# First mixer of a two-block transformer: attention heads, gate chunks and branch product interleaved in rounds

## The chip, the cores and the metric

One core of one Trainium2 chip runs the whole program in one launch. The metric is the device time of that execution in microseconds (us); three executions of the kernel before took 1167.99 to 1169.90 us, with a median of 1169.39 us.

## The reference, cut to what matters

The input is one sequence of 256 tokens by 1024 channels, all in float32. Two blocks follow one another. The change touches only the mixer of the first block:

```python
z, xbc, dt_raw, q, k, v, gate_logits = split(u @ w_in)
y_ssd = ssd_branch(z, xbc, dt_raw, ...)              # ends in (256 x 2048) @ ssd_w_branch (2048 x 1024)
s = (q_m @ k_m.T) * scale - slope[h] * distance      # 8 heads, two maps m, causal
p = softmax(s)
out = (p[0] - lam * p[1]) @ v                        # per head, 256 x 128
y_att = rmsnorm(out, subln_g) * (1 - lam_init) @ da_w_branch
gates = sigmoid(gate_logits + gate_b)                # 2 x 1024 columns
merged = gates[0] * y_ssd + gates[1] * y_att
h = h + rmsnorm(merged @ w_out, mix_post_g)
```

## The kernel before

Tokens lie in two tiles of 128 (t = 0, 1). Every large matrix product is made with operands split in a high and a low part and three matmuls per tile (`parts`, L1479 to L1481), each 128x128 by 128x512. The weights come in units of 128x2048 elements (1 MB) through a ring of five slots. For each unit the queue of SyncE issues a load, once the unit five before it is used (`w_used`). ScalarE then copies the high part (`split_hi`, L437) and VectorE subtracts it to get the low part (`split_lo`, L913). Both engines take the units in order, at places written out by hand in their programs. TensorE waits for `w_lo`. One unit is 24 matmuls, 12 for each tile. In this document a block is one such group of 12.

Nothing plans the order at run time: each engine has one program and works through it in order, and semaphores tie them together.

In the stretch that the change touches, before its first line, the ring has 71 units split on both engines, and units 66 and 67 (gate chunk 0) are already multiplied and kept. Then come, in the kernel before:

- the eight differential heads, one per step of a loop (`for h in range(9)`, L658 on ScalarE, L1168 on VectorE, L1720 on TensorE). VectorE adds the distance table and takes maxima (L1178 to L1182, "max" below), ScalarE takes the exponentials (L670, "exp"), VectorE normalizes and subtracts the two maps (L1190 to L1198, "diff"), TensorE turns the result (three transposes, L1726), ScalarE copies it (L661, "keep"), TensorE multiplies by V (L1739 to L1741, "values"), VectorE copies the result out (`o_keep`, L1165) and ScalarE squares it (L679). The map `SMAP`, the buffer `ATT`, the copy `PT` and the bank `PS[6]` exist once each.
- in the same steps, the SSD branch product: eight units of `ssd_w_branch`, one per head. The operand is turned by TensorE into `PS[7]` (four transposes, L1619), split by `kt_hi` (L530) and `kt_lo` (L1002), and multiplied by `rows` with both tiles (24 matmuls in one go).
- after the heads, the gate chunks 1 to 3, two units each, in one go each. VectorE adds the bias (L1248), ScalarE takes the sigmoid (L694), and VectorE multiplies the SSD branch by its gate into `V` (`first_merge`, L1212).
- then the attention branch's four units (`by_pairs(8, U_DAW, ...)`), the second merge, and `w_out`'s four units.

On ScalarE a head's step is: keep, `kt_hi`, `split_hi`, exp, squares. On VectorE it is: `kt_lo`, max, `split_lo`, `o_keep`, diff. So ScalarE splits before it waits for the maxima of the head.

A later part of the kernel, the second block's mixer, has its own sixteen heads in a loop of 18 rounds (`for q in range(18)`), where three heads are under way at once and a block of 12 matmuls stands between the scores of one head and the values of another. There the VectorE splits stand mostly one round behind those of ScalarE.

Of the kernel before, what the change touches and what calls it, by code (L numbers as in the profile page):

```python
# [113 lines left out]
CHUNK[U_GATE0] = len(CHUNK)  # L114
CHUNK.update({U_GATE + 2 * i: len(CHUNK) + i for i in range(3)})
# [69 lines left out]
def program(nc, w, out):  # L185
    with ExitStack() as ctx:
# [238 lines left out]
        def _(act):  # L425
# [229 lines left out]
            kt_hi(0, 0)  # L655


            for h in range(9):  # L658
                if h:
                    act.wait_ge(p_turned, h)  # L660
                    nc.scalar.activation(PT, PS[6][:, 0:384], ACT.Copy).then_inc(p_kept, 1)  # L661
                if h < 8:
                    if h:
                        kt_hi(h, U_SSDW + h - 1)
                        split_hi()
                    act.wait_ge(s_ready, h + 1)
                    for m in range(2):
                        for i, ks in enumerate((slice(0, P), slice(P, 3 * P))):
                            n = 2 * i + m
                            ins = nc.scalar.activation(SMAP[:, m, ks], SMAP[:, m, ks], ACT.Exp, scale=0.125,  # L670
                                                       bias=SM[:, 4 + n:5 + n], accum_out=SM[:, 8 + n:9 + n])
                            if i == 0:
                                own.inc(ins)
                        ins.then_inc(p_exp, 1)
                if h:
                    act.wait_ge(o_kept, h)
                    for i in range(NT):
                        own.wait()
                        own.inc(nc.scalar.activation(SQJ[:, i * P:(i + 1) * P], XN[:, i, (h - 1) * P:h * P], ACT.Square,  # L679
                                                     accum_out=SS[:, i * 8 + h - 1:i * 8 + h]))  # L680
            split_hi()
            rsqrt(RS[:], SS[:], 1, o_rs, 1.0 / P)


            nc.scalar.preload_act_table(ACT.Sigmoid)
            for n in range(4):
                if n == 3:
                    kt_hi(8, U_DAW - 1, SUBLN)
                if n:
# [210 lines left out]
        def _(dve):  # L900
# [257 lines left out]
            kt_lo(0)  # L1158
# [9 lines left out]
            for h in range(9):  # L1168
                if h < 8:
                    if h:  # L1170
                        kt_lo(h)

                    dve.wait_ge(scores, h + 1)
                    if h:
                        own.wait()
                    f = -8.0 * slopes[h]
                    for m in range(2):
                        own.inc(stt(SMAP[:, m, :], tab("dist"), f, PS[4 + m][:, 0:384], ALU.mult, ALU.add))  # L1178
                    own.wait()
                    own.inc(nc.vector.tensor_reduce(SM[:, 0:2], SMAP[:, :, 0:P], AX.X, ALU.max))  # L1180
                    own.link(nc.vector.tensor_reduce(SM[:, 2:4], SMAP[:, :, P:3 * P], AX.X, ALU.max))
                    ts(SM[:, 4:8], SM[:, 0:4], -0.125, None, ALU.mult).then_inc(s_ready, 1)  # L1182
                    if h:
                        split_lo()
                if h:
                    o_keep(h - 1)
                if h < 8:

                    dve.wait_ge(p_exp, 2 * (h + 1))
                    own.link(nc.vector.reciprocal(SM[:, 12:16], SM[:, 8:12]))  # L1190
                    own.link(ts(SM[:, 16:20], SM[:, 12:16], SM[:, 39:40], None, ALU.mult))

                    if h:
                        dve.wait_ge(p_turned, h)
                    own.inc(ts(ATT[:, 0:P], SMAP[:, 0, 0:P], SM[:, 12:13], None, ALU.mult))
                    own.link(ts(ATT[:, P:3 * P], SMAP[:, 0, P:3 * P], SM[:, 14:15], None, ALU.mult))
                    own.inc(stt(ATT[:, 0:P], SMAP[:, 1, 0:P], SM[:, 17:18], ATT[:, 0:P], ALU.mult, ALU.add))
                    stt(ATT[:, P:3 * P], SMAP[:, 1, P:3 * P], SM[:, 19:20], ATT[:, P:3 * P], ALU.mult,  # L1198
                        ALU.add).then_inc(attn_ok, 1)
                    dve.wait_ge(attn_ok, h + 1)  # L1200
# [12 lines left out]

            def second_merge(m, gates, unit):

                def product(b):
                    g = slice(D + (b % 2) * 512, D + (b % 2) * 512 + 512)
                    if m:
                        own.inc(stt(MB[:, b, :], gates[:, b // 2, g], 1.0, PS[b][:], ALU.add, ALU.mult))
                    else:  # L1220
                        own.inc(tt(MB[:, b, :], PS[b][:], gates[:, b // 2, g], ALU.mult))
# [9 lines left out]
                kt_lo(20 if m else 12, 0.5 if m else None)  # L1231
# [7 lines left out]
            for n in range(4):  # L1239
                if n == 3:  # L1240
                    kt_lo(8, SUBLN)
                if n == 0:
                    dve.wait_ge(gate0_kept, 2)
                cols = slice(n * 512, (n + 1) * 512)
                for t in range(NT):
                    if n:
                        chunk_tile(gate_unit(n), gate_unit(n) + 1, t)
                    tt(BUF1[:, t, cols], PS[gate_bank(n, t)][:] if n else BUF1[:, t, cols], GAIN[:, cols],  # L1248
                       ALU.add).then_inc(g_logit, 1)
                if n:  # L1250
                    split_lo()
                    split_lo()
                if n == 2:

                    dve.wait_ge(gates_ok, 2)
                    for b in range(4):
                        first_merge(BUF1, b, acc_read)
# [4 lines left out]
            products(12, U_WOUT, 4, turned=True)  # L1262
# [766 lines left out]
```

## Time and profile before

| | us |
|---|---|
| median of three executions | 1169.39 |
| the profiled execution, its own time | 1170.61 |
| its span, first to last instruction | 1168.8 |
| PE busy in the span | 1123.3 |
| VectorE (DVE) busy | 694.4 |
| ScalarE (ACT) busy | 586.1 |
| stretch that the change touches, last gate 0 matmul to attention branch's first matmul | about 439.5 to 546.2 |

PE is the matmul part of TensorE and PEld its weight load. A group's row gives the start, the duration and in brackets how long the engine sat idle before it and which engine's work ended that. Matmuls overlap one another in this profile: each lasts 0.39 us in the rows and the next begins 0.23 us after it, so that the work of a stretch on PE is read from the starts, and a wait shows as a start that comes later than 0.23 us. The profile's lines are those of the kernel before.

### The profile page before, as it was taken

Reading aid. Unit: us, or ns where it says so; the run is one execution under the profiler, and the core shown is the slowest. Engines: PE = TensorE matmul, PEld = TensorE weight load, DVE = VectorE, ACT = ScalarE, POOL = GpSimd, SP = SyncE. Lnnn points to the kernel's source line nnn. Section 1 sums busy time; section 2 is a strip of 40 time slices with the busy share of each in tenths; the row PEclk is TensorE's granted clock in tenths of the full one; section 3 lists DMA queues with packets and bytes.
Section 4 is the critical chain, followed back from the end, with each engine's and each line's share of the span. In section 5 each row is a group of like instructions: output and inputs, shape, how many; then the busy total and the mean of one; then the engine's idle time right before and its main releaser. Section 6 shows DMA issues by size and latency. Waiting matters only on the chain. (4 is left out here: it accounts for less than half of the span.)

```text
span 1168.8 us, 13926 instructions
## 1 busy us (share of the span) xinstructions
PE 1123.3 (96%) x5748; PEld 942.0 (81%) x5748; DVE 694.4 (59%) x793; ACT 586.1 (50%) x828; POOL 21.4 (2%) x35
## 2 busy tenths in 40 slices
PE   5999999999999999999999999999899999999997
PEld 4888887899989986777778888877778877888886
DVE  4644554676767777776666445446665656555443
ACT  4543434554567765664455434345566535343333
POOL 0000000000001110000000000000000000000000
PEclk9999999899999999999999999999999999999999
DMA  9656653655566544445456565554633345566550
GB/s 306 213 180 189 195 193 115 218 179 180 176 188 199 185 154 167 143 123 184 146 185 210 183 195 195 183 152 140 203 109 126 131 139 182 181 191 197 187 180 36
DMA packets 132206, 202.74 MB, mean 173 GB/s; under 512 B 5760, under 2 KB 98816, under 8 KB 131888
## 3 DMA queue, kind: packets, MB, share of 16 engines
q1 hardware_dynamic: 129328, 190.68, 50.6%
q0 software_dynamic: 2816, 11.18, 2.8%
q8 instruction: 46, 0.75, 0.3%
q14 instruction: 16, 0.13, 0.0%
HBM read 200.76 MB, written 1.08 MB: 173 GB/s over the span
## 5 line engine op out<-in xcount | busy, mean ns | idle before, releaser
L913 DVE TENSOR_TENSOR WL<-RAW,WH 128x2048 fp32r<-128x2048 f32 (+1 forms) x181 | 406.2, 2265 | 111.1 <-ACT WH L437 111.1
L437 ACT ACTIVATE WH<-RAW 128x2048 fp32r<-128x2048 f32 (+1 forms) x181 | 338.5, 1888 | 12.6 <-DMA RAW<-in_w_out 3.7
L1479 PE MATMUL PS<-WH,XTH 128*128 128x512 f32 (+1 forms) x676 | 267.3, 395 | 0.0
L1481 PE MATMUL PS<-WH,XTL 128*128 128x512 f32 (+1 forms) x676 | 263.4, 390 | 0.0
L1480 PE MATMUL PS<-WL,XTH 128*128 128x512 f32 (+1 forms) x676 | 262.8, 389 | 0.0
L1479 PE MATMUL ACC<-WH,KTH 128*128 128x512 f32 (+1 forms) x476 | 188.7, 396 | 5.7 <-DVE WL L913 3.5
L1481 PE MATMUL ACC<-WH,KTL 128*128 128x512 f32 (+1 forms) x476 | 185.8, 390 | 0.0
L1480 PE MATMUL ACC<-WL,KTH 128*128 128x512 f32 (+1 forms) x476 | 185.4, 390 | 0.0
L1481 PEld LDWEIGHTS PS<-WH,XTL 128*128 128x128 f32 x676 | 126.8, 188 | 26.5
L1479 PEld LDWEIGHTS PS<-WH,XTH 128*128 128x128 f32 x676 | 127.0, 188 | 24.9 <-issue 0.5
L1480 PEld LDWEIGHTS PS<-WL,XTH 128*128 128x128 f32 x676 | 127.1, 188 | 24.6
L1479 PEld LDWEIGHTS ACC<-WH,KTH 128*128 128x128 f32 x476 | 89.8, 189 | 26.2 <-DVE WL L913 6.8
L1481 PEld LDWEIGHTS ACC<-WH,KTL 128*128 128x128 f32 x476 | 89.7, 188 | 18.7
L1480 PEld LDWEIGHTS ACC<-WL,KTH 128*128 128x128 f32 x476 | 89.8, 189 | 17.4
L477 ACT ACTIVATE KTH<-PS 128x512 fp32r<-128x512 f32 x33 | 19.7, 597 | 164.2 <-PE PS L1539 164.0
L935 DVE TENSOR_TENSOR KTL<-PS,KTH 128x512 fp32r<-128x512 f32 x33 | 22.8, 690 | 122.0 <-ACT KTH L477 122.0
L487 ACT ACTIVATE SCR<-PS 128x256 f32<-128x256 f32 x66 | 25.3, 384 | 121.3 <-PE PS L1481 121.2
L944 DVE TENSOR_TENSOR SCR<-PS,SCR 128x256 f32<-128x256 f32 x66 | 27.6, 421 | 54.5 <-ACT SCR L487 54.4
L1479 PE MATMUL ACC<-XTH,WH 128*128 128x256 f32 x192 | 55.9, 291 | 0.0
L1480 PE MATMUL ACC<-XTL,WH 128*128 128x256 f32 x192 | 55.4, 288 | 0.0
L1481 PE MATMUL ACC<-XTH,WL 128*128 128x256 f32 x192 | 55.3, 288 | 0.0
L1479 PE MATMUL ACC<-WH,XTH 128*128 128x512 f32 (+1 forms) x120 | 47.5, 396 | 1.9 <-ACT SCR L720 1.9
(264 smaller groups left out, 1283.0 us busy)
## 6 DMA issues: line engine op xcount, KB each, us to landing
RAW<-in_w_in SPq DMA_DIRECT2D x50, 1024.0 KB, 5.2
RAW<-in_ffn_w_gate SPq DMA_DIRECT2D x44, 512.0 KB, 4.0
RAW<-in_ffn_w_up SPq DMA_DIRECT2D x44, 512.0 KB, 5.0
RAW<-in_ffn_w_down SPq DMA_DIRECT2D x22, 1024.0 KB, 4.9
RAW<-in_w_gate SPq DMA_DIRECT2D x22, 512.0 KB, 4.0
RAW<-in_w_up SPq DMA_DIRECT2D x22, 512.0 KB, 5.0
RAW<-in_w_down SPq DMA_DIRECT2D x11, 1024.0 KB, 4.9
RAW<-in_ssd_w_branch SPq DMA_DIRECT2D x8, 1024.0 KB, 5.0
```

Of the source, the lines that this page charges most:

```text
L437: nc.scalar.activation(WH[:, s, 0:n], RAW[:, s, 0:n], ACT.Copy).then_inc(w_hi, 1)
L477: nc.scalar.activation(KTH[:, half_of(j)], PS[6][:], ACT.Copy).then_inc(hT_hi, 1)
L487: nc.scalar.activation(SG[:, t, :], PS[4 + t][:, 0:256], ACT.Silu).then_inc(gate_ok, 1)
L913: tt(WL[:, s, 0:n], RAW[:, s, 0:n], WH[:, s, 0:n].bitcast(F32), ALU.subtract).then_inc(w_lo, 1)
L935: tt(KTL[:, half_of(j)], PS[6][:], KTH[:, half_of(j)].bitcast(F32), ALU.subtract).then_inc(hT_lo, 1)
L944: tt(HS[:, t, :], PS[4 + t][:, 256:512], SG[:, t, :], ALU.mult).then_inc(h_ready, 1)
L1479: mm(ps, stat_hi, mov_hi, start=first, stop=False)
L1480: mm(ps, stat_hi, mov_lo, start=False, stop=False)
L1481: return mm(ps, stat_lo, mov_hi, start=False, stop=last)
```

## The change

The eight heads go into ten rounds, q = 0 to 9, written out by hand. In round q the scores of head q are made, its maxima and exponentials taken; the diff of head q-1 and its transposes; the values, `o_keep` and squares of head q-2. Between these steps stand the blocks of 12 matmuls of gate chunks 1 and 2 (rounds 0 to 2) and of the SSD branch product (rounds 3 to 8). That product now goes by tile in eight steps (two blocks each, over pairs of units, as `by_pairs` does), with operand steps `ssd_turn`, `ssd_kt_hi`, `kt_lo`. Gate chunk 3 follows the heads. The weight units are loaded in the new order: gates 0 to 2, SSD branch, gate 3. The sigmoid becomes (1 + tanh(x/2))/2: the additions of 1 are made in the merges, which were multiplications, and the factor 0.5 is taken in the splits of the operand of `w_out`. The first merge writes over the gates instead of into `V`. The scaling of the attention result by its norm is four instructions instead of one.

The diff, cut: the bodies of the steps on the heads are the old ones under names (`head_max1`, `head_exp1`, `head_diff1`, `head_keep1`, `head_square1`, `head_scores1`, `head_values1`) and are left out, as are most of the removed lines, which stand in the kernel before. The order is ScalarE, VectorE, TensorE.

```diff
-U_SSDW = U_GATE0 + 2
-U_GATE = U_SSDW + 8
-U_DAW = U_GATE + 6
+U_GATE = [U_GATE0, U_GATE0 + 2, U_GATE0 + 4]
+U_SSDW = U_GATE[2] + 2
+U_GATE += [U_SSDW + 8]
+U_DAW = U_GATE[3] + 2
 U_WOUT = U_DAW + 4
...
-return ((4, 0), (4, 5), (6, 7), (4, 5))[n][t]
+return ((4, 0), (1, 7), (2, 3), (4, 5))[n][t]
...
+def ssd_kt_hi(s):
+    if s >= 2 and s % 2 == 0:
+        act.wait_ge(tile_half, HALF[U_SSDW + s - 2])
+    kt_hi(s, U_SSDW + s - 1 if s % 2 else 0)
+def gate_tanh(n, count):
+    act.wait_ge(g_logit, count)
+    a = BUF1[:, :, n * 512:(n + 1) * 512]
+    nc.scalar.activation(a, a, ACT.Tanh, scale=0.5).then_inc(gates_ok, 1)
...
+nc.scalar.preload_act_table_set("exp_and_others")
+for q in range(10):
+    if q < 8:
+        head_exp1(q)
+    if q == 0:
         split_hi()
         split_hi()
+    elif q in (1, 6, 7, 8):
+        split_hi()
+    elif q == 2:
+        split_hi()
+        gate_tanh(1, 2)
+        ssd_kt_hi(0)
+    elif q == 3:
+        split_hi()
+        ssd_kt_hi(1)
+        gate_tanh(2, 4)
+    elif q == 4:
+        ssd_kt_hi(2)
+        split_hi()
+        ssd_kt_hi(3)
+    elif q == 5:
+        split_hi()
+        gate_tanh(0, 6)
+        ssd_kt_hi(4)
+        split_hi()
+    if q == 6:
+        ssd_kt_hi(5)
+        ssd_kt_hi(6)
+    elif q == 7:
+        ssd_kt_hi(7)
+    if q >= 2:
+        if q == 9:
+            ln_exp()
+            split_hi()
+        head_square1(q - 2)
+    if 1 <= q <= 8:
+        head_keep1(q - 1)
+rsqrt(RS[:], SS[:], 1, o_rs, 1.0 / P)
+nc.scalar.preload_act_table_set("exp_and_others")
+act.wait_ge(tile_half, HALF[U_SSDW + 6])
+kt_hi(8, U_DAW - 1, SUBLN)
+split_hi()
+gate_tanh(3, 8)
+split_hi()
 products(8, U_DAW, 4, SUBLN, True)
 act.wait_ge(tile_half, HALF[U_DAW + 2])
+kt_hi(12, U_DAW, 0.5)
 split_hi()
+products(12, U_WOUT, 4, 0.5, turned=True)
...
+def head_diff1(h):
+    dve.wait_ge(p_exp, 2 * (h + 1))
+    own.link(nc.vector.reciprocal(SM[:, 12:16], SM[:, 8:12]))
+    own.link(ts(SM[:, 16:20], SM[:, 12:16], SM[:, 39:40], None, ALU.mult))
+    if h:
...
+def ssd_merge(t):
+    dve.wait_ge(gates_ok, 3)
+    dve.wait_ge(w_used, U_SSDW + 8) if t else dve.wait_ge(tile_half, HALF[U_SSDW + 6])
+    for h in range(2):
+        a = BUF1[:, t, h * 512:(h + 1) * 512]
+        stt(a, a, 1.0, PS[2 * t + h][:], ALU.add, ALU.mult).then_inc(acc_read, 1)
+for q in range(10):
+    if 1 <= q <= 8:
+        head_diff1(q - 1)
+    if q < 8:
+        head_max1(q)
+    if q == 0:
+        split_lo()
+        split_lo()
+    elif q == 1:
+        dve.wait_ge(gain_loaded, 48)
+        gate_add(1)
+        split_lo()
+    elif q == 2:
+        split_lo()
+        kt_lo(0)
+    elif q == 3:
+        gate_add(2)
+        split_lo()
+        kt_lo(1)
+    elif q == 4:
+        kt_lo(2)
+        split_lo()
+        gate_add(0)
+        kt_lo(3)
+    elif q == 5:
+        split_lo()
+        kt_lo(4)
+    elif q == 6:
+        kt_lo(5)
+        split_lo()
+        kt_lo(6)
+        split_lo()
+    elif q == 7:
+        split_lo()
+        kt_lo(7)
+    elif q == 8:
+        split_lo()
+        ssd_merge(0)
+    elif q == 9:
+        ssd_merge(1)
+    if q >= 2:
+        o_keep(q - 2)
 split_lo()
 dve.wait_ge(o_rs, 1)
+for p in range(2):
+    for t in range(NT):
+        o4 = XN[:, t, p * 512:(p + 1) * 512].rearrange("p (h c) -> p h c", c=P)
+        tt(o4, o4, RS[:, t * 8 + 4 * p:t * 8 + 4 * p + 4].unsqueeze(2).to_broadcast([P, 4, P]),
+           ALU.mult).then_inc(o_ok, 1)
+kt_lo(8, SUBLN)
+split_lo()
+gate_add(3)
+split_lo()
...
+def gate_piece(n, h, t):
+    c = U_GATE[n] + h
+    pe.wait_ge(w_lo, c + 1)
+    ins = half(c, h, t, gate_bank(n, t))
+    if t:
+        ins.then_inc(w_used, 1)
+    elif h:
+        ins.then_inc(chunk_half, 1)
+def ssd_turn(s):
+    turn_tile(s, BUF2, 4 * (s // 2), s % 2)
+def ssd_piece(s, i):
+    pe.wait_ge(k_lo, s + 1)
+    pair_rows(U_SSDW + s // 2 * 2, i, s % 2, s % 2, s < 2, s >= 6)
...
+def head_turn1(h):
+    pe.wait_ge(attn_ok, h + 1)
+    if h:
+        pe.wait_ge(o_kept, h)
...
+pe.wait_ge(qkv_kept, 10)
+gate_piece(1, 0, 0)
+pe.wait_ge(qkv_kept, 12)
+pe.wait_ge(gate0_kept, 1)
+head_scores1(0)
+gate_piece(1, 0, 1)
+gate_piece(1, 1, 0)
+gate_piece(1, 1, 1)
+head_scores1(1)
+pe.wait_ge(ssd_cbm, 8)
+gate_piece(2, 0, 0)
+pe.wait_ge(y_gated, 8)
+gate_piece(2, 0, 1)
+head_turn1(0)
+head_scores1(2)
+gate_piece(2, 1, 0)
+head_values1(0)
+gate_piece(2, 1, 1)
+pe.wait_ge(ys_ok, 8)
+pe.wait_ge(g_logit, 2)
 pe.wait_ge(gate0_kept, 2)
+ssd_turn(0)
+head_turn1(1)
+head_scores1(3)
+ssd_piece(0, 0)
+head_values1(1)
+ssd_turn(1)
+ssd_piece(0, 1)
+pe.wait_ge(g_logit, 4)
+ssd_piece(1, 0)
+head_turn1(2)
+for q in (4, 6):
+    s = (1, 4)[q // 6]
+    head_scores1(q)
+    ssd_turn(s + 1)
+    ssd_piece(s, 1)
+    head_values1(q - 2)
+    ssd_piece(s + 1, 0)
+    ssd_turn(s + 2)
+    ssd_piece(s + 1, 1)
+    head_turn1(q - 1)
+    if q == 4:
+        head_scores1(5)
+        ssd_piece(3, 0)
+        head_values1(3)
+        ssd_turn(4)
+        ssd_piece(3, 1)
+        ssd_piece(4, 0)
+        head_turn1(4)
+head_scores1(7)
+ssd_piece(6, 0)
+head_values1(5)
+ssd_turn(7)
+ssd_piece(6, 1)
+head_turn1(6)
+ssd_piece(7, 0)
+head_values1(6)
+ssd_piece(7, 1)
+head_turn1(7)
+pe.wait_ge(s_ready, 8)
+gate_piece(3, 0, 0)
+head_values1(7)
+gate_piece(3, 0, 1)
+gate_piece(3, 1, 0)
+pe.wait_ge(o_ok, 1)
+turn_tile(8, XN, 0, 0)
+gate_piece(3, 1, 1)
+pe.wait_ge(acc_read, 2)
 def first_merged():
     pe.wait_ge(merged, 1)
+    turn_tile(12, BUF1, 0, 0)
+def heads_ready(s):
+    pe.wait_ge(o_ok, (1, 2, 3, 4)[s])
+    if s == 1:
+        pe.wait_ge(acc_read, 4)
+by_pairs(8, U_DAW, XN, ready=heads_ready, turned=True, then=first_merged)
+by_pairs(12, U_WOUT, BUF1, ready=lambda s: pe.wait_ge(merged, (1, 3, 2, 4)[s]), turned=True)
```

## Rows read from the trace of the kernel before

**Rows 1.** Page, busy time by engine, share of the span, instruction count.

```profile
PE 1123.3 (96%) x5748; PEld 942.0 (81%) x5748; DVE 694.4 (59%) x793; ACT 586.1 (50%) x828; POOL 21.4 (2%) x35
```

**Rows 2.** Timeline of PE, one head's step: start, duration, engine, line, operation.

```profile
456.62 0.39 PE L1481 MATMUL ACC<-WH,KTL 128*128 128x512 f32 x1
457.20 0.55 PE L1726 MATMUL PS<-TAB,SCR 128*128 128x128 f32 x3 [0.20 <-DVE SCR L1198]
457.68 0.50 PE L1733 MATMUL PS<-QK 64*128 64x128 f32 x4
...
458.54 0.49 PE L1739 MATMUL PS<-V,SCR 128*128 128x128 f32 x2
...
459.09 0.39 PE L1741 MATMUL PS<-V,SCR 128*128 128x128 f32 x2
459.61 0.66 PE L1619 MATMUL PS<-TAB,BUF 128*128 128x128 f32 x4
460.02 0.48 PE L1479 MATMUL ACC<-WH,KTH 128*128 128x512 f32 x1
```

**Rows 3.** Timeline of PE, both ends of the stretch.

```profile
439.30 0.39 PE L1481 MATMUL ACC<-WH,XTL 128*128 128x512 f32 x1
...
546.27 0.39 PE L1479 MATMUL ACC<-WH,KTH 128*128 128x512 f32 x1
```

**Rows 4.** Timeline of DVE and ACT, one head's step.

```profile
449.82 1.92 ACT L437 ACTIVATE WH<-RAW 128x2048 fp32r<-128x2048 f32 x1
450.64 1.01 DVE L1178 SCALAR_TENSOR_TENSOR SCR<-TAB,PS 128x384 f32<-128x384 f32 x2
452.81 2.28 DVE L913 TENSOR_TENSOR WL<-RAW,WH 128x2048 fp32r<-128x2048 f32 x1
452.94 0.40 ACT L670 ACTIVATE SCR<-SCR,SM 128x128 f32<-128x128 f32 x1 [1.20 <-DVE SM L1182]
...
454.62 0.19 ACT L670 ACTIVATION_READ_ACCUMULATOR SCR<-SCR,SM 128x1 f32 x1
455.01 0.42 DVE L1165 COPY XN<-PS 128x256 f32<-128x256 f32 x1
455.35 0.17 DVE L1190 RECIPROCAL SM<-SM 128x4 f32<-128x4 f32 x1
456.67 0.48 DVE L1198 SCALAR_TENSOR_TENSOR SCR<-SCR,SM 128x256 f32<-128x256 f32 x1
```

**Rows 5.** Timeline of ACT and DVE, the operand's two splits.

```profile
458.17 0.59 ACT L530 ACTIVATE KTH<-PS 128x512 fp32r<-128x512 f32 x1
458.87 0.69 DVE L1002 TENSOR_TENSOR KTL<-PS,KTH 128x512 fp32r<-128x512 f32 x1 [1.72 <-ACT KTH L530]
```

**Rows 6.** Timeline of ACT and DVE, the one split that follows directly on the other.

```profile
513.57 1.90 ACT L437 ACTIVATE WH<-RAW 128x2048 fp32r<-128x2048 f32 x1
515.50 2.29 DVE L913 TENSOR_TENSOR WL<-RAW,WH 128x2048 fp32r<-128x2048 f32 x1 [2.71 <-ACT WH L437]
```

**Rows 7.** Timeline of PE, one block of 12 matmuls between two other steps, second mixer.

```profile
868.82 0.50 PE L1479 MATMUL ACC<-WH,XTH 128*128 128x512 f32 x1
...
871.70 0.33 PE L1875 MATMUL PS<-BUF,GAIN 128*128 128x64 f32 x2
```

**Rows 8.** Timeline of DVE and ACT, gate steps and a table load.

```profile
515.84 1.28 ACT L685 ACT_TABLE_LOAD   x1
543.75 0.69 DVE L1248 TENSOR_TENSOR BUF<-PS,GAIN 128x512 f32<-128x512 f32 x1 [1.19 <-PE PS L1481]
547.19 1.06 ACT L694 ACTIVATE BUF<-BUF 128x1024 f32<-128x1024 f32 x1 [1.81 <-DVE BUF L1248]
```

**Rows 9.** Engines around two waits: us, PE, PEld, DVE, ACT, POOL, PEclk, DMA, GB/s.

```profile
576.00:578.00 2.00, 2.00 (x7) 1.60 (x6) 2.00 (x1) 0.00 (x0) 0.00 (x0) 0.62 0.00 0
578.00:580.00 2.00, 2.00 (x6) 1.57 (x5) 2.00 (x2) 0.00 (x0) 0.00 (x0) 0.52 0.00 0
833.00:834.00 1.00, 0.00 (x0) 0.00 (x0) 0.93 (x8) 1.00 (x4) 0.00 (x0) 1.00 0.68 158
```

More of the change, by code:

```diff
@@ L113 @@
 CHUNK.update({U_QKV + 8 + 2 * i: len(CHUNK) + i for i in range(2)})
-CHUNK[U_GATE0] = len(CHUNK)
-CHUNK.update({U_GATE + 2 * i: len(CHUNK) + i for i in range(3)})
+CHUNK.update({u: len(CHUNK) + i for i, u in enumerate(U_GATE)})
 CHUNK.update({U_FFN2 + FF_AT["a", j]: len(CHUNK) + j for j in range(FF_STEPS)})
@@ L654, in _ @@
                     u += 1
[L655 to L689, printed above, removed]
+            def ssd_kt_hi(s):
[6 more added lines that the diff above has]
+                nc.scalar.activation(a, a, ACT.Tanh, scale=0.5).then_inc(gates_ok, 1)
@@ new lines, in head_exp1 @@
+            def head_exp1(h):
+                act.wait_ge(s_ready, h + 1)
+                for m in range(2):
+                    for i, ks in enumerate((slice(0, P), slice(P, 3 * P))):
+                        n = 2 * i + m
+                        ins = nc.scalar.activation(SMAP[:, m, ks], SMAP[:, m, ks], ACT.Exp, scale=0.125,
+                                                   bias=SM[:, 4 + n:5 + n], accum_out=SM[:, 8 + n:9 + n])
+                        if i == 0:
+                            own.inc(ins)
+                    ins.then_inc(p_exp, 1)
@@ new lines, in head_keep1, with head_square1 @@
+            def head_keep1(h):
+                act.wait_ge(p_turned, h + 1)
+                nc.scalar.activation(PT, PS[6][:, 0:384], ACT.Copy).then_inc(p_kept, 1)
+            def head_square1(h):
+                act.wait_ge(o_kept, h + 1)
+                for i in range(NT):
+                    own.wait()
+                    own.inc(nc.scalar.activation(SQJ[:, i * P:(i + 1) * P], XN[:, i, h * P:(h + 1) * P], ACT.Square,
+                                                 accum_out=SS[:, i * 8 + h:i * 8 + h + 1]))
@@ L1157, in _ @@
                     split_lo()
-            kt_lo(0)
             slopes = [2.0 ** (-8.0 * (h + 1) / DA_HEADS) for h in range(DA_HEADS)]
@@ L1166, in o_keep @@
                                       PS[6][:, 0:256].rearrange("p (i c) -> p i c", i=NT)).then_inc(o_kept, 1)
-            dve.wait_ge(ys_ok, 8)
[L1168 to L1200, printed above, removed]
@@ new lines, in head_max1 @@
+            def head_max1(h):
+                dve.wait_ge(scores, h + 1)
+                own.wait()
+                f = -8.0 * slopes[h]
+                for m in range(2):
+                    own.inc(stt(SMAP[:, m, :], tab("dist"), f, PS[4 + m][:, 0:384], ALU.mult, ALU.add))
+                own.wait()
+                own.inc(nc.vector.tensor_reduce(SM[:, 0:2], SMAP[:, :, 0:P], AX.X, ALU.max))
+                own.link(nc.vector.tensor_reduce(SM[:, 2:4], SMAP[:, :, P:3 * P], AX.X, ALU.max))
+                ts(SM[:, 4:8], SM[:, 0:4], -0.125, None, ALU.mult).then_inc(s_ready, 1)
@@ L1217, in product @@
                     g = slice(D + (b % 2) * 512, D + (b % 2) * 512 + 512)
[L1218 to L1221, printed above, removed]
+                    own.inc(stt(MB[:, b, :], gates[:, b // 2, g], 1.0, PS[b][:], ALU.add, ALU.mult))
                 def add(b):
-                    v = (BUF2 if m else V)[:, b // 2, (b % 2) * 512:(b % 2 + 1) * 512]
+                    v = gates[:, b // 2, (b % 2) * 512:(b % 2 + 1) * 512]
                     tt(v, v, MB[:, b, :], ALU.add).then_inc(merged, 1)
@@ L1230, in second_merge @@
                     add(b)
-                kt_lo(20 if m else 12, 0.5 if m else None)
+                kt_lo(20 if m else 12, 0.5)
                 dve.wait_ge(w_used, unit + 1)
@@ L1238, in second_merge @@
                 add(3)
[L1239 to L1257, printed above, removed]
             products(8, U_DAW, 4, SUBLN, True)
@@ L1261, in _ @@
             second_merge(0, BUF1, U_DAW + 3)
-            products(12, U_WOUT, 4, turned=True)
+            products(12, U_WOUT, 4, 0.5, turned=True)
             boundary(1, U_WOUT + 3, 4)
@@ new lines, in head_scores1 @@
+            def head_scores1(h):
+                if h:
+                    pe.wait_ge(s_ready, h)
+                for m in range(2):
+                    ms = slice(m * 64, (m + 1) * 64)
+                    mm(PS[4 + m][:, 0:P], QK[ms, h, 0, 0:P], QK[ms, h, 1, 0:P], start=True, stop=True)
+                    ins = mm(PS[4 + m][:, P:3 * P], QK[ms, h, 0, P:TOK], QK[ms, h, 1, :], start=True, stop=True)
+                ins.then_inc(scores, 1)
+            def head_turn1(h):
+                pe.wait_ge(attn_ok, h + 1)
+                if h:
+                    pe.wait_ge(o_kept, h)
+                for b in range(3):
+                    ins = nc.tensor.transpose(PS[6][:, b * P:(b + 1) * P], ATT[:, b * P:(b + 1) * P], IDENT)
+                ins.then_inc(p_turned, 1)
```

91 lines of the change are left out of this document (26 added, 65 removed).

## The prediction

> **What bounds the kernel now.** I read the page first. PE is busy for 96% of the span, DVE for 59% and ACT for 50% [rows 1]. So the only gain that is left is PE's waits, and what counts is whether the two other engines hand over in time, not how full they are. Then I read PE's timeline through one head's step. The last matmul of a block starts at 456.62, so the next step could start at 456.85; it starts at 457.20, when the diff is ready. The values' last pass starts at 459.09, and the operand's turn could follow 0.22 later, at 459.31; it starts at 459.61, when `kt_lo` has ended (458.87 + 0.69 = 459.56) [rows 2, 5]. So a step holds about 0.65 us of wait in 8.8.
>
> The whole stretch runs from 439.30 to 546.27, or 107.0 us [rows 3]. Its work on PE: 28 blocks of 12 matmuls at 0.2275 each, 76.4, and 0.2 for the matmul at 439.30; eight heads at 0.48 (transposes, 457.20 to 457.68), 0.86 (scores, to 458.54) and 0.77 (values, to 459.31), 16.9; nine turns at 0.41 (459.61 to 460.02), 3.7; and a break of 0.15 wherever a block begins behind something else, read from the second mixer, where one block takes 871.70 - 868.82 = 2.88 against 2.73 [rows 2, 7]. The old order has ten breaks, 1.5. Together 98.7, so PE waits 8.3 in the stretch. This is the most that the change can win here.
>
> **The change on PE.** No matmul is added or removed. The blocks now stand in 22 groups instead of ten: 12 breaks more, +1.8 us on the path. The float32 forms of the other steps stay.
>
> **The change on DVE and ACT.** Durations from one head's step: max 450.64 to 452.90, 2.26 (ACT's exp begins 0.04 behind it); exp 452.94 to 454.81, 1.87; diff 455.35 to 457.15, 1.80, of which 0.45 come before its wait for the transposes of the head before, and 1.35 behind it; `o_keep` 0.42; `split_hi` 1.92; `split_lo` 2.28 [rows 4]. `kt_hi` 0.59 and `kt_lo` 0.69 [rows 5]. A `split_lo` starts 0.03 after the `split_hi` of its unit, if it has to wait for it [rows 6]. A bias add is 0.69 per tile, a gate function 1.06 [rows 8].
>
> The step that decides is where the splits stand. In the old step ACT splits a unit at 449.82, ahead of its exp, and DVE, done with max at 452.81, begins its half at once [rows 4]. In the new rounds ACT has exp first and the split behind it, in every round but the fourth, and DVE has the same unit in the same round, right behind max (I counted: 71 units on both before the heads, then 71 and 72 in round 0, 73 in round 1, and so on). So behind max DVE waits for exp and `split_hi`, 3.8 us, less what stands there. Behind that `split_lo` stand `kt_lo` and, last in the round, `o_keep`. PE's `head_turn1(q-1)` at the end of round q waits for the `o_keep` of round q, and behind it in PE's queue are the next scores, for which the next max waits. Each round is thus one chain: transposes 0.5, rest of diff 1.35, max 2.3, exp 1.9, `split_hi` 1.9, `split_lo` 2.3, `kt_lo` 0.65, `o_keep` 0.4, about 11.3 us. PE's own work in a round is 8.3 with two blocks and 11.1 to 11.6 with three.
>
> I laid the three orders side by side from 439.5 with these durations. Times are of the old span.
> Round 0: scores 442.4 (behind one gate block), max to 445.6, exp to 447.5, both `split_hi` to 451.15, both `split_lo` to 453.9. Round 1: diff, max to 457.95, exp to 459.85, `split_hi` to 461.7, `split_lo` to 464.0. PE has gate blocks and doesn't wait yet. Round 2: diff, max to 468.05, exp, `split_hi` to 471.8, tanh, `kt_hi(0)` to 473.35, `kt_lo(0)` to 474.8, `o_keep(0)` to 475.15. PE stands at `head_turn1(1)` from 466.35 to 475.2: **8.85 us**. Round 3: max to 479.4, exp, split pair to 485.45, `kt_lo(1)` to 486.1; PE wants it at 483.5: 2.65. Round 4: scores 489.5, max to 493.25, exp, `kt_hi(2)`, `kt_lo(2)` to 496.45; PE wants it at 494.45: 2.05. Round 5: max to 506.9, exp, split pair to 512.95, `kt_lo(4)` to 513.6, wanted at 511.0: 2.65. Round 6: max to 520.75, exp, `split_hi`, `kt_hi(5)`, `kt_lo(5)` to 525.7, wanted at 521.95: 3.8; then two units and `kt_lo(6)` put `o_keep(4)` at 533.3, wanted at 531.95: 1.4. Round 7: split pair to 543.6, `kt_lo(7)`, `o_keep(5)` to 544.65, wanted at 541.65: 3.05. Round 8: 0.2. Gate 3 then covers the last head. Its bias add comes behind its last block, ACT's tanh(3) behind that, then a split pair, and only then `kt_hi(9)` and `kt_lo(9)`, about 574.4, which the attention branch's second tile wants at 571.1: 3.35. The waits sum to 28.0.
>
> So the sum is 28.0 + 1.8 - 8.3 = +21.5 us. Loads don't bind: the closest is unit 77, whose slot is free at about 489 and whose split is due at 509. The gate bias is loaded by GpSimd as before, and lies ready before round 1. Tanh for sigmoid, additions in the merges and the factor 0.5 change no instruction by more than 0.1. The four scalings for one (2.5 for 2.3) and the load of `mix_post_g`, now about 20 us later, are covered by gate 3 and by the attention branch.
>
> **Table loads.** The change needs two more (exp set back in, ln set out), 1.28 each [rows 8]. One lies ahead of the first exp, for which ACT waits until max is done at 445.6. The two in round 9 lie before the norm of the heads, which is ready about 1.3 before PE asks for it. So: nothing. The Trainium skill (ScalarE: Activation LUTs, What ACT_TABLE_LOAD costs) adds a drain of 1.38 to each 1.28; the norm would then be just late and the sum would rise by about 1. The row of the trace shows 1.28, and the rest of the sum doesn't use the page.
>
> **The clock.** After a wait at 574 to 576, PE's clock was 0.62 and 0.52 over the next 4 us, which is half speed for 3.4 us and costs (0.38 + 0.48) x 2 = 1.7 us; after the wait around 833 to 834 it stayed at 1.00 [rows 9]. Of the new waits, seven are 2 us or more. After some the slow stretch is eaten by the next wait for DVE (behind the 8.85, for one), after others, where the next max hangs on PE (rounds 5, 6, 7), it lies on the path. I take two, 3.4; none and six (10.2) are the bounds. Forecast: +21.5 + 3.4 = +24.9. The profiled execution took 1170.6, 1.8 over its span; the sum against it is 1195.5, and the median of the runs shown lies 1.2 below it. So 1194.3.
>
> **The rivals.**
> PE stays fed, the other side: the queues of DVE and ACT run far enough ahead, as in the second mixer, so that the blocks cover the heads. Then 8.3 are won and 1.8 lost: 1163. It decides itself at `head_turn1(1)`: if `o_keep(0)` were ready by then. For it: the load on each engine is small [rows 1]. Against it: in round 2 there are 10 us of strictly ordered steps behind the diff, which PE has 2 blocks to cover. 5%.
> Only the rounds with two blocks wait: if the chains are shorter by a couple of us than I have them (splits that don't wait for each other, a PE break that is longer), the three-block rounds hide them. 8.85 + 3.05 + 3.35 + 1.8 - 8.3 = +8.8, so 1178. For it: my waits in rounds 3 to 5 are near 2. 15%.
> The clock falls after each long wait, all on the path: +21.5 + 10.2, so 1201. 17%. The Trainium skill (TensorE: Matmul & The Clock Gate, HAM oscillation) tells of such a kernel, in which every wait between bursts of matmuls is followed by a stretch at the lower clock. The two places in rows 9 say once yes and once no.
> The forecast has 60%; the rest, 3%, is something not seen, at no change or nearby.
>
> **How the numbers follow.** The likeliest is 1194.3. Its own range is 1189 to 1198 (clock none to three, 2 us of error over eight chains). With the second and third rival on either side: 1178 to 1202. A measurement of this kernel tells 0.2%, 2.3 us, from no change. Faster 5% (first rival), same 2%, slower 93%.
>
> **What would show it.** In the profile after: PE waits of about 9 us once, at the transposes of head 1, released by DVE's copy L1165 or what it is called then; waits of 2 to 4 us before the SSD blocks, released by the operand's low part; `split_lo` rows whose idle time ends with ACT's `split_hi`, in nearly every round, 2 to 4 us each; rounds of 11 to 13 us. The stretch to the first block of the attention branch lasts 125 to 129 us instead of 107. Wrong would be rounds of 8.3 us where two blocks stand, or a first long wait for something else.

## The result, and the profile after

The changed kernel takes 1197.6 us (1194.7 to 1203.4), the one before 1169.6: a ratio of 1.0247, 95% interval 1.0213 to 1.0281. The profiled execution took 1197.25, its span is 1195.5; against the span of before, 1168.8, that is 26.7 more. The page, busy time by engine, the clock's row and the group of the low splits:

```profile
PE 1130.2 (95%) x5748; PEld 949.0 (79%) x5748; DVE 695.1 (58%) x796; ACT 588.1 (49%) x830; POOL 21.4 (2%) x35
PEclk9999999899999998989999999999999999999999
L953 DVE TENSOR_TENSOR WL<-RAW,WH 128x2048 fp32r<-128x2048 f32 (+1 forms) x181 | 406.3, 2265 | 133.4 <-ACT WH L435 133.4
```

TensorE has the same 5748 matmuls as in rows 1, but is busy 6.9 us longer: the same work at a lower clock in places. VectorE and ScalarE have as much work as before (0.7 and 2.0 us more). VectorE's idle time ahead of the low splits, 133.4 us, was 111.1 before. So the time is in waiting, and after it in the clock. TensorE's waits by cause over the span (us in all, times, longest):

```profile
PE PS L1819 <- DVE XN L1202: 13.4, 3, 8.9
PE ACC L1548 <- DVE KTL L1042: 8.6, 3, 3.8
PE ACC L1548 <- DVE KTL L1044: 3.4, 1, 3.4
```

L1819 is `head_turn1`, L1202 is `o_keep`, L1042 and L1044 are `kt_lo`. Where they lie, TensorE's timeline (the last number is the idle time before the row):

```profile
474.87 0.87 PE L1819 MATMUL PS<-TAB,SCR 128*128 128x128 f32 x3 [8.87 <-DVE XN L1202]
...
486.45 0.47 PE L1548 MATMUL ACC<-WH,KTH 128*128 128x512 f32 x1 [0.70 <-issue]
...
496.65 0.50 PE L1548 MATMUL ACC<-WH,KTH 128*128 128x512 f32 x1 [2.02 <-DVE KTL L1042]
...
515.23 0.80 PE L1548 MATMUL ACC<-WH,KTH 128*128 128x512 f32 x1 [2.78 <-DVE KTL L1042]
...
528.67 0.79 PE L1548 MATMUL ACC<-WH,KTH 128*128 128x512 f32 x1 [3.82 <-DVE KTL L1042]
...
537.73 0.52 PE L1819 MATMUL PS<-TAB,SCR 128*128 128x128 f32 x3 [1.32 <-DVE XN L1202]
...
549.10 0.87 PE L1819 MATMUL PS<-TAB,SCR 128*128 128x128 f32 x3 [3.18 <-DVE XN L1202]
...
569.65 0.39 PE L1548 MATMUL ACC<-WH,KTH 128*128 128x512 f32 x1
...
579.09 0.51 PE L1548 MATMUL ACC<-WH,KTH 128*128 128x512 f32 x1 [3.35 <-DVE KTL L1044]
...
603.79 0.50 PE L1548 MATMUL ACC<-WH,KTH 128*128 128x512 f32 x1 [1.87 <-DVE WL L953]
```

The row at 569.65 answers to 546.27 in rows 3: the attention branch's first block comes 23.4 us later. The last gate 0 matmul of the changed kernel starts at 439.10 (439.30 before), so the stretch lasts 130.6 us for 107.0. One more wait, 3.35, lies behind it. The last row is a wait for `w_out`'s unit that was there before, 1.88 long:

```profile
575.39 0.50 PE L1479 MATMUL ACC<-WH,KTH 128*128 128x512 f32 x1 [1.88 <-DVE WL L913]
```

Why the first one lasts 8.87 us is read on the two other engines, round 2 (L1215 ends max, L671 is exp, L435 `split_hi`, L663 tanh, L528 `kt_hi`, L953 `split_lo`):

```profile
467.61 0.17 DVE L1215 TENSOR_SCALAR SM<-SM 128x4 f32<-128x4 f32 x1
467.81 0.40 ACT L671 ACTIVATE SCR<-SCR,SM 128x128 f32<-128x128 f32 x1 [6.01 <-DVE SM L1215]
469.58 1.89 ACT L435 ACTIVATE WH<-RAW 128x2048 fp32r<-128x2048 f32 x1
471.38 1.04 ACT L663 ACTIVATE BUF<-BUF 128x1024 f32<-128x1024 f32 x1
471.50 2.29 DVE L953 TENSOR_TENSOR WL<-RAW,WH 128x2048 fp32r<-128x2048 f32 x1 [3.73 <-ACT WH L435]
472.32 0.57 ACT L528 ACTIVATE KTH<-PS 128x512 fp32r<-128x512 f32 x1
473.71 0.68 DVE L1042 TENSOR_TENSOR KTL<-PS,KTH 128x512 fp32r<-128x512 f32 x1
474.31 0.41 DVE L1202 COPY XN<-PS 128x256 f32<-128x256 f32 x1
```

ScalarE first stands idle for 6.01 us, then does exp and the split one behind the other, while VectorE stands idle for 3.73 us. Neither of the two overlaps with work of VectorE; only tanh and `kt_hi` do. In rows 4 the split at 449.82 lies ahead of exp, beside max, and VectorE starts on it at once. The clock around the waits (us, PE, PEld, DVE, ACT, POOL, PEclk, DMA, GB/s):

```profile
466.00:468.00 2.00, 0.00 (x0) 0.00 (x0) 1.71 (x5) 0.19 (x1) 0.00 (x0) 1.00 0.66 129
...
472.00:474.00 2.00, 0.00 (x0) 0.00 (x0) 2.00 (x2) 0.90 (x2) 0.00 (x0) 0.50 0.00 0
...
478.00:480.00 2.00, 2.00 (x7) 1.52 (x6) 1.93 (x6) 0.24 (x1) 0.00 (x0) 0.50 0.00 0
...
498.00:500.00 2.00, 2.00 (x6) 1.61 (x5) 2.00 (x2) 0.00 (x0) 0.00 (x0) 0.50 0.18 68
...
604.00:606.00 2.00, 2.00 (x10) 1.62 (x10) 2.00 (x2) 0.35 (x1) 0.00 (x0) 1.00 0.00 0
```

At 0.50, half speed, the row counts 6 matmuls in 2 us, at 1.00 it counts 10 (with those that run across an edge). The clock falls within the idle time of 8.87 and stays at half until about 481. It falls in the same way behind five more waits, those of 2.02, 2.78, 3.82, 3.18 and 3.35, for 1.7 us worth of work each (behind the 2.02: 0.95, 0.50 and 0.70 in three windows of 2 us). Behind the `w_out` wait at 603.79 it stays whole, where it fell before [rows 9]. Behind the next wait, 1.59 us long and ended at 625.69, it falls again (0.88, 0.50 and 0.77 from 626 to 632), as it does in the kernel before behind the same wait, 1.57 us long and ended at 598.89 (0.60 and 0.55 from 600 to 604).

### The profile page after: what moved, and what is told of

Same layout as the page of the kernel before. It is cut to its first block and busy times, and to the rows that moved or that the text cites. A ratio compares the mean times of both kernels' runs of the same rounds, so it can differ in the third digit from the quotient of the medians.

```text
span 1195.5 us, 13938 instructions
## 1 busy us (share of the span) xinstructions
PE 1130.2 (95%) x5748; PEld 949.0 (79%) x5748; DVE 695.1 (58%) x796; ACT 588.1 (49%) x830; POOL 21.4 (2%) x35
## 5 line engine op out<-in xcount | busy, mean ns | idle before, releaser
L953 DVE TENSOR_TENSOR WL<-RAW,WH 128x2048 fp32r<-128x2048 f32 (+1 forms) x181 | 406.3, 2265 | 133.4 <-ACT WH L435 133.4
L435 ACT ACTIVATE WH<-RAW 128x2048 fp32r<-128x2048 f32 (+1 forms) x181 | 338.8, 1889 | 11.8 <-DMA RAW<-in_ffn_w_up 3.9
L1548 PE MATMUL PS<-WH,XTH 128*128 128x512 f32 (+1 forms) x652 | 258.8, 397 | 0.0
L1550 PE MATMUL PS<-WH,XTL 128*128 128x512 f32 (+1 forms) x652 | 254.4, 390 | 0.0
L1549 PE MATMUL PS<-WL,XTH 128*128 128x512 f32 (+1 forms) x652 | 253.6, 389 | 0.0
L1548 PE MATMUL ACC<-WH,KTH 128*128 128x512 f32 (+1 forms) x476 | 193.1, 406 | 18.2 <-DVE KTL L1042 8.6
L1550 PE MATMUL ACC<-WH,KTL 128*128 128x512 f32 (+1 forms) x476 | 188.7, 396 | 0.0
L1549 PE MATMUL ACC<-WL,KTH 128*128 128x512 f32 (+1 forms) x476 | 188.2, 395 | 0.0
L1550 PEld LDWEIGHTS PS<-WH,XTL 128*128 128x128 f32 x652 | 122.4, 188 | 25.7
L1548 PEld LDWEIGHTS PS<-WH,XTH 128*128 128x128 f32 x652 | 122.6, 188 | 24.0 <-issue 0.7
L1549 PEld LDWEIGHTS PS<-WL,XTH 128*128 128x128 f32 x652 | 122.8, 188 | 23.5
L1548 PE MATMUL ACC<-WH,XTH 128*128 128x512 f32 (+1 forms) x144 | 57.0, 396 | 1.9 <-ACT SCR L760 1.9
```

The source lines that it names most:

```text
L435: nc.scalar.activation(WH[:, s, 0:n], RAW[:, s, 0:n], ACT.Copy).then_inc(w_hi, 1)
L953: tt(WL[:, s, 0:n], RAW[:, s, 0:n], WH[:, s, 0:n].bitcast(F32), ALU.subtract).then_inc(w_lo, 1)
L1548: mm(ps, stat_hi, mov_hi, start=first, stop=False)
L1549: mm(ps, stat_hi, mov_lo, start=False, stop=False)
L1550: return mm(ps, stat_lo, mov_hi, start=False, stop=last)
```

## The experiments

The theory: the rounds are one chain, in which the split behind exp puts VectorE's half, `kt_lo` and `o_keep` late. Rivals: `o_keep` is late because it is last in VectorE's order; the order of TensorE itself costs; the gates as tanh cost. The clock is a question of its own. Each kernel was timed in three rounds against the kernel before.

**Splits ahead of exp.** On ScalarE, in rounds 0 to 8:

```diff
 for q in range(10):
+    if q == 0: split_hi()
+    if q < 9:  split_hi()
     if q < 8:  head_exp1(q)
-    if q == 0: split_hi(); split_hi()
-    elif q in (1, 6, 7, 8): split_hi()
     ...        # rounds 2 to 5: their first split_hi gone
```

> The changed kernel, with one edit: in rounds 0 to 8 ScalarE splits its unit before it waits for the maxima of the head, not behind the exponentials. Units, rounds and all else stay. Theory A (the split behind exp holds VectorE, and with it kt_lo and o_keep, for 3.8 us in each round): by the durations of the rows of before, the waits of TensorE fall from 28.0 us to about 10.5 (2.05 at the transposes of head 1, 1.9 and 1.85 at the operand's low part in rounds 4 and 6, 1.4 in round 6, 3.35 at the second tile of the attention branch), most of the stretches at half clock go too: 1173 to 1178 us. Theory B (what holds TensorE is o_keep as the last step of VectorE's round): o_keep stays last, so a gain of at most 4 us: 1193 to 1197. Theory C (the interleaving itself costs, more switches between kinds of matmul and more semaphores): no change, about 1197.

1175.3 us, ratio 1.0041 (1.0023 to 1.0059), span 1173.3. Moving ten calls gives back 22.3 of the 28.0 us. Between the two profiled executions the spans differ by 22.2 us, of which 20.9 lie in the stretch (109.7 us for 130.6). TensorE's timeline of it:

```profile
467.22 0.52 PE L1814 MATMUL PS<-TAB,SCR 128*128 128x128 f32 x3 [1.83 <-DVE XN L1197]
...
486.91 0.50 PE L1543 MATMUL ACC<-WH,KTH 128*128 128x512 f32 x1 [2.02 <-DVE KTL L1037]
...
511.61 0.50 PE L1543 MATMUL ACC<-WH,KTH 128*128 128x512 f32 x1 [2.02 <-DVE KTL L1037]
...
520.75 0.52 PE L1814 MATMUL PS<-TAB,SCR 128*128 128x128 f32 x3 [1.34 <-DVE XN L1197]
...
557.55 0.79 PE L1543 MATMUL ACC<-WH,KTH 128*128 128x512 f32 x1 [3.35 <-DVE KTL L1039]
```

The 8.87 is down to 1.83, the waits of rounds 3, 5 and 7 are gone, and the five that stay have a step of their own in front: `kt_lo` ahead of `o_keep` in round 2, `kt_hi` behind exp in rounds 4 and 6, a second split in round 6, and tanh(3) and two splits in the tail. VectorE's idle time ahead of the low splits falls from 133.4 to 113.5 us, near the 111.1 of the kernel before. The waits of the stretch and its tail fall from 26.0 to 10.6 us in sum; the rest of the gain in the stretch is the half clock behind them. This chain is shown as the main cause.

**`o_keep` early.** On VectorE `o_keep(q - 2)` stands right behind `head_max1(q)`:

```diff
     if q < 8: head_max1(q)
+    if q >= 2: o_keep(q - 2)
     ...
-    if q >= 2: o_keep(q - 2)
```

> The changed kernel, with one edit: VectorE's o_keep of head q-2 stands right behind the maxima of head q in each round, ahead of the split and kt_lo. Theory A (split behind exp): the wait at the transposes of head 1 shrinks from 8.9 to about 2, but about 5 of it comes back before the first block of the SSD product, for which kt_lo(0) is as late as before; 1.4 in round 6 goes, 3.05 in round 7 becomes about 2.2: in all 3 to 5 us faster, 1192 to 1195. Theory B (o_keep last): the three waits that VectorE's copy ends (8.9, 1.3, 3.2 us) go, and with them what they hold up: 12 to 15 us faster, 1182 to 1186. Theory C: no change.

1193.7 us, ratio 1.0206 (1.0189 to 1.0223). The wait doesn't go, it changes its name:

```profile
468.45 0.52 PE L1819 MATMUL PS<-TAB,SCR 128*128 128x128 f32 x3 [2.23 <-DVE XN L1202]
...
474.65 0.79 PE L1548 MATMUL ACC<-WH,KTH 128*128 128x512 f32 x1 [4.82 <-DVE KTL L1042]
...
547.51 0.50 PE L1548 MATMUL ACC<-WH,KTH 128*128 128x512 f32 x1 [3.23 <-DVE KTL L1042]
```

The trace of the changed kernel names `o_keep` as releaser of the longest wait. With it out of the way, TensorE waits for `kt_lo` instead, which hangs on the same split.

**Tanh alone.** The kernel before with its gates as tanh, its additions and its factors of 0.5, in the old order:

> The kernel before, with the arithmetic of the change alone: gates as tanh of half the logit, 1 added in the merges, 0.5 in the splits of the operand of w_out, the set of exp loaded in place of that of sigmoid. All theories of the order: no difference from the kernel before, within 0.2% (1167 to 1172). If the arithmetic or the table had a share in the 28 us, this is slower by that share.

1169.1 us, ratio 1.0000 (0.9991 to 1.0010). This part costs nothing, which leaves the order.

**VectorE a unit behind.** Instead of moving ScalarE's splits, VectorE splits one unit less in round 0 and one more in round 9, so that in each round it takes the unit of the round before:

```diff
     if q == 0:
         split_lo()
-        split_lo()
 ...
     elif q == 9:
+        split_lo()
         ssd_merge(1)
```

> The changed kernel, with one edit: VectorE splits in each round the unit that ScalarE has split in the round before (one unit in round 0, one more in round 9), so that it never waits for ScalarE's split of the same round; ScalarE's order stays, so that kt_hi still comes behind exp and the split. Theory A in its full form (kt_hi too is held by the split on ScalarE, and kt_lo, o_keep with it): about half of the gain of the first experiment, waits of 18.5 us instead of 28.0, 1184 to 1189 us. If the wait of VectorE for the split were all of it, it would be as fast as the first experiment (1173 to 1178). Theories B and C: no change, 1195 to 1198.

1188.8 us, ratio 1.0170 (1.0144 to 1.0196). The number lies in the range of the first theory, but partly for a reason that I had not worked out. The waits that it was to shorten are shorter (3.24 for 8.87, and no wait for `kt_lo` is over 2.02 in the heads), and a new one, by far the largest, stands in round 6, in TensorE's and VectorE's timelines:

```profile
522.11 0.77 PE L1548 MATMUL ACC<-WH,KTH 128*128 128x512 f32 x1 [9.53 <-DVE WL L953]
...
519.08 0.69 DVE L1042 TENSOR_TENSOR KTL<-PS,KTH 128x512 fp32r<-128x512 f32 x1 [4.21 <-ACT KTH L528]
519.68 2.28 DVE L953 TENSOR_TENSOR WL<-RAW,WH 128x2048 fp32r<-128x2048 f32 x1
```

`ssd_piece(4, 1)` needs a unit that this order splits only in round 6, behind `kt_lo(5)`, and that waits 4.21 us for `kt_hi(5)`, which ScalarE has behind exp and split. So this run says that the lag of one unit takes the first waits away, and nothing sharper: its total is a sum of two effects, and the agreement with the expected range is chance in part.

**The rest of the waits.** The splits ahead of exp, and five moves more in the orders of ScalarE and VectorE, each for one of the waits left above:

```diff
 # ScalarE, rounds 4 and 6
     split_hi()
+    ssd_kt_hi(2)          # 5 in round 6; was behind exp
     head_exp1(q)
 # VectorE, round 2, and likewise o_keep(4) in round 6
     split_lo()
+    o_keep(0)
     kt_lo(0)
 # ScalarE, tail
     kt_hi(8, U_DAW - 1, SUBLN)
     split_hi()
-    gate_tanh(3, 8)
     split_hi()
+    kt_hi(9, U_DAW, SUBLN)
+    gate_tanh(3, 8)
 # VectorE, tail
     gate_add(3)
+    kt_lo(9, SUBLN)
     split_lo()
```

> The whole computation, the splits of e1_split_first, and five more moves in ScalarE's and VectorE's orders: o_keep(0) ahead of kt_lo(0) in round 2; kt_hi(2) and kt_hi(5) ahead of exp in rounds 4 and 6; o_keep(4) ahead of round 6's second split_lo; behind the heads kt_hi(9) ahead of tanh(3) and kt_lo(9) ahead of the next split_lo. TensorE's order is the one of the change. Theory A (the waits come from the order in the two other queues alone, and the half clock comes from the waits): in e1_split_first the waits at these places are 1.83, 2.02, 2.02, 1.34 and 3.35, together 10.6 us, and the clock is near half for 1.7 us worth behind three of them (468-472, 512-518, 556-562), 5.1. Without both, less some 0.5 for what is late next: 1175.3 - 15.2 = 1160, so 1158 to 1165, faster than the kernel before; no wait above 1 us on TensorE between 440 and 560. Rival B (a wait that is moved comes back a step later, since the units' splits then come late): 1168 to 1174. Rival C (interleaving itself costs more than it gives, by its 12 breaks): not under 1169, even with all waits gone.

1162.1 us (1160.9 to 1163.5), ratio 0.9933 (0.9916 to 0.9949), span 1161.7. It beats both kernels, the one before by 0.7%. TensorE's order is that of the change, to the matmul. Its timeline, and the two windows around the wait for `w_out`:

```profile
475.80 0.47 PE L1557 MATMUL ACC<-WH,KTH 128*128 128x512 f32 x1 [1.20 <-issue]
...
521.16 0.52 PE L1828 MATMUL PS<-TAB,SCR 128*128 128x128 f32 x3 [0.78 <-DVE XN L1205]
...
540.62 0.39 PE L1557 MATMUL ACC<-WH,KTH 128*128 128x512 f32 x1
...
569.52 0.50 PE L1557 MATMUL ACC<-WH,KTH 128*128 128x512 f32 x1 [1.87 <-DVE WL L956]
```

```profile
568.00:570.00 2.00, 0.48 (x2) 0.43 (x3) 2.00 (x3) 2.00 (x2) 0.00 (x0) 1.00 0.57 198
570.00:572.00 2.00, 2.00 (x11) 1.62 (x10) 2.00 (x2) 0.09 (x1) 0.00 (x0) 1.00 0.00 0
```

Two waits above 0.3 us are left in the stretch, and the clock is whole all the way. The first block of the attention branch starts at 540.62, 5.7 us ahead of the 546.27 in rows 3. The span is 7.1 shorter; the other 1.4 are the half clock behind the `w_out` wait, which is not there. These 1.4 us are no merit of the order: the wait is as long as before (1.87 for 1.88). The rival that said interleaving costs more than it gives has fallen. One expectation here was missed: a wait of 1.20 is above the 1 us that I had set. Which of the five moves gives how much was not run one by one; that they are worth about 13 together is (11.6 between the profiled executions).

**Filling the waits.** The clock by itself: the changed kernel with identity products on TensorE, float32, 128x128, results unused, placed in the long waits.

```diff
+def fill(n, bank=4, heads=0):
+    if heads: pe.wait_ge(s_ready, heads)
+    for _ in range(n):
+        mm(PS[bank][:, 0:P], IDENT, IDENT, start=True, stop=True)
 ...
     ssd_turn(0)
+    fill(37, 0)
     head_turn1(1)
```

> The changed kernel with matmuls added into TensorE's waits, nothing else: 128x128 float32 products of the identity, results unused, at 0.22 us each, 37 ahead of the transposes of head 1 (wait of 8.87), then 10, 8, 11, 15, 12 and 13 at the waits of 0.70 (2.65 if the clock were whole), 2.02, 2.78, 3.82, 3.18 and 3.35. They end before what TensorE waits for, so no work is moved; only the engine is busy in the wait. Own theory (the half clock behind the waits costs time on the path, more than the 3.4 us I put down): the granted clock stays at 1.00 from 470 to 584, the stretch to the attention branch's first block falls from 130.3 us to 125, and the time from 1197.6 to 1188-1193. The sum of the prediction without its term for the clock, 1190.9, lies in there. Rival (the slow stretches are eaten by the next wait for VectorE): the clock is whole, but the time stays at 1195-1198. Second rival (the clock falls for another reason than idle time): it still falls at the same places, time 1197 or more.

1190.3 us, ratio 1.0176 (1.0161 to 1.0191), span 1189.5. TensorE has 106 products more, some 24 us of work, and the kernel is 7.3 us faster; the stretch, from each kernel's own last gate 0 matmul (439.39 and 439.10), is 124.4 us long for 130.6. Its timeline, and the only windows from 440 to 600 with a clock below 0.99:

```profile
475.16 0.52 PE L1828 MATMUL PS<-TAB,SCR 128*128 128x128 f32 x3 [0.59 <-DVE XN L1202]
...
513.40 0.50 PE L1548 MATMUL ACC<-WH,KTH 128*128 128x512 f32 x1 [0.30 <-DVE KTL L1042]
...
525.45 0.50 PE L1548 MATMUL ACC<-WH,KTH 128*128 128x512 f32 x1 [0.48 <-DVE KTL L1042]
...
544.37 0.52 PE L1828 MATMUL PS<-TAB,SCR 128*128 128x128 f32 x3 [0.52 <-DVE XN L1202]
...
573.27 0.50 PE L1548 MATMUL ACC<-WH,KTH 128*128 128x512 f32 x1 [0.44 <-DVE KTL L1044]
596.38 0.50 PE L1548 MATMUL ACC<-WH,KTH 128*128 128x512 f32 x1 [1.87 <-DVE WL L953]
```

```profile
596.00:598.00 2.00, 1.62 (x6) 1.35 (x7) 2.00 (x3) 0.94 (x1) 0.00 (x0) 0.87 0.02 5
598.00:600.00 2.00, 2.00 (x6) 1.54 (x6) 2.00 (x2) 0.00 (x0) 0.00 (x0) 0.50 0.00 0
```

Set against the same rows of the changed kernel, this prices each dip on the path. At the transposes of head 1 the filled kernel is 0.3 late, as it was when the stretch began. It is then early by 0.3 at round 4's wait (496.65 to 496.37), by 1.8 at round 5's wait (515.23 to 513.40), by 3.2 at round 6's (528.67 to 525.45), by 4.7 at round 7's (549.10 to 544.37), by 5.8 at the tail's (579.09 to 573.27) and by 7.4 at `w_out` (603.79 to 596.38). The first dip thus cost 0.6 on the path, and each of the five of 1.7 between 1.1 and 1.6, together 7.7. At `w_out` the filled kernel has the half clock that the changed one hasn't, and ends 6.0 ahead. So it is shown that the clock stays whole here when the waits are filled, and that the half clock lies on the path. That idle time is the only thing that lowers the clock is not shown (last section).

How it comes onto the path is seen on VectorE. Behind the slow stretch of round 5 its diff waits for TensorE's transposes of the head before (the changed kernel, then the filled one):

```profile
520.08 0.28 DVE L1224 TENSOR_SCALAR SCR<-SCR,SM 128x128 f32<-128x128 f32 x1 [4.23 <-PE PS L1819]
...
516.86 0.29 DVE L1224 TENSOR_SCALAR SCR<-SCR,SM 128x128 f32<-128x128 f32 x1 [2.83 <-PE PS L1828]
```

L1819 and L1828 are both `head_turn1`. With the whole clock the wait is 1.4 us shorter.

## Why the prediction was right

**The waits.** The sign, the mechanism and the place were right. Each wait against its forecast: 8.87 for 8.85, 2.02 for 2.05, 2.78 for 2.65, 3.82 for 3.8, 1.32 for 1.4, 3.18 for 3.05, 3.35 for 3.35. Round 2's steps on the two other engines came within 0.5 us of the order laid out. The sign on the low splits held in rounds 0 to 3, 5 and 7, where they wait 2.54 to 3.74 us for ScalarE's half; in rounds 4 and 8 it is about 1, and in round 6 `kt_lo(5)` waits in their place, 4.21. The sign "rounds of 11 to 13 us" was set too narrow: from the end of one max to the next it is 10.1 us in round 1, 13.8 to 15.2 in rounds 3 to 5, and 18.3 in round 6 with its second unit, and the layout itself had 13.85 in round 3. One wait was missed in size, round 3's, 0.70 for 2.65: the half clock behind the 8.87 slowed TensorE by 2.9 us there, which used up 1.95 of the wait. The forecast had said that this one would be eaten.

**The interleaving.** The sum had 98.7 of work and 1.8 for twelve breaks: 100.5 us for a stretch without waits. The kernel with all moves takes 540.62 - 439.41 = 101.2, with waits of 1.20, 0.78 and 0.26 in it, so about 99.0 of work: the two terms together were 1.5 too high. The first rival had 6.5 us to win, and the stretch is 5.8 shorter. So its time, 1163, is about what the order gives once the queues are fed (1162.1 measured, with the 1.4 of clock at `w_out` in it); it was no forecast for this change, whose queues are not.

**The clock, mis-sized.** The term was 3.4, two dips on the path. Six long waits were followed by half clock, and the filled kernel shows 7.7 us of it on the path, less 1.4 because the dip at `w_out` was gone: 6.3, or 2.9 more than the term. The rest of the sum was 0.8 too high: the filled kernel's span is 20.7 us over that of the kernel before, for +21.5. So the spans differ by 26.7 for 24.9 forecast. The medians differ by 28.0, since the profiled execution of before was 1.0 above its median and that of the changed kernel 0.3 below its own.

The step that failed is "I take two": in rounds 4 to 7 and in the tail the next piece of VectorE's chain waits for TensorE's own work (the diff for `head_turn1`, L1224 above; the next `kt_lo`, by way of `kt_hi`, for the operand's turn: the second one of round 6 waits 3.55 us for 2.03 in the filled kernel), so each slow stretch delays the chain too. The stretch came out at 130.6 for this reason, just over the 125 to 129 of the forecast. That 1197.6 still lies within the narrower range, 1189 to 1198, is partly luck: with half clock behind `w_out`, as before, it would be 1199 by this estimate. The bound for six, 10.2, was too high by what round 3 ate and by the 0.1 to 0.6 that was lost of each. The third rival (1201) was right that the clock falls after each long wait, and too high in that all of it lies on the path: 7.7 for its 10.2. What the Trainium skill tells of a kernel (TensorE: Matmul & The Clock Gate, HAM oscillation), that each wait between bursts of matmuls is followed by the lower clock, is nearly so in this trace: six of the seven waits of 1.87 us and more that the changed kernel has here are followed by half clock.

**Tables and tanh.** Free, as costed: tanh alone gave 1.0000, and the two loads of round 9 (558.23 and 562.96, 1.28 each) lie beside TensorE's gate chunk 3. No row shows a drain beside them: ScalarE's work before the first ends at 557.73 + 0.49 = 558.22, and its next split starts at 559.53, 0.02 after the load. TensorE doesn't wait for the norm. The second rival (only two-block rounds wait, 1178) fell by the waits of 2.02 and 2.78 in rounds 4 and 5.

## What to carry to other kernels

When a loop is software-pipelined over three in-order engines, write down for each round the longest run of steps that hand over to one another; every step that needs nothing from the current item (here the weight splits) goes ahead of the first step that waits for it, on both engines. Here ten moved calls on one queue were worth 22 us, more than all that the new order of matmuls could win. Price a TensorE wait of 2 us and more at its length and, where what comes next hangs on TensorE, some 1.5 us of half clock with it; as the next section shows, this price is that of the changed kernel and no rule.

## What the runs showed of the hardware that was not expected

The same wait can cost the clock or not. The one for `w_out` is 1.87 or 1.88 us long in all eight kernels. Half clock follows it in five, the kernel before [rows 9], tanh alone, `o_keep` early, VectorE a unit behind, and the filled one (596 to 600 above), and not in the changed one, with the splits ahead of exp, or with all moves (568 to 572 above). Likewise of the two waits of 2.02 us with the splits ahead of exp, the one before 511.61 is followed by it and the one before 486.91 is not. Longer waits can pass too: with `o_keep` early the clock stays at 1.00 behind those of 2.35 (485.34), 2.02 (495.57) and 3.23 us (547.51), while around those of 2.78 (512.59) and 3.81 (527.43) it is at half for some 6.8 us each, twice as long as behind the waits of the changed kernel.

Nor does it take a wait. In the changed kernel TensorE has no idle row from 216 to 232, and the clock is at half from about 224.7 to 231.6:

```profile
220.65 0.26 PE L1549 MATMUL ACC<-WL,XTH 128*128 128x32 f32 x1
...
226.00:228.00 2.00, 2.00 (x11) 2.00 (x11) 1.37 (x6) 0.46 (x2) 0.00 (x0) 0.50 0.19 19
```

What TensorE did just before are matmuls 32 columns wide, from 220.29 on. The clock falls at this place in all eight kernels. What decides it stays open. It also shows in the spread: the shortest execution of the changed kernel (span 1192.9) had a mean granted clock of 0.984, the longest (1201.6) of 0.974. Unneeded matmuls, 24 us of them over seven waits, made a kernel 7.3 us faster.
